# Four value pages of the last group between the passes of the scores in a hybrid decoder step

## The reference

```python
s_past = jnp.einsum('bqhd,bkhd->bhqk', q, k_past) * scale + g[..., :, None] + suffix[..., None, :]
s_new = jnp.einsum('bqhd,bkhd->bhqk', q, k) * scale + g[..., :, None] - g[..., None, :]
s_new = jnp.where(causal, s_new, -jnp.inf)
p = jax.nn.softmax(jnp.concatenate([s_past, s_new], axis=-1), axis=-1)
return einsum('bhqk,bkhd->bqhd', p[..., :n_past], v_past) + einsum('bhqk,bkhd->bqhd', p[..., n_past:], v)
```

## Time and profile before

| | us |
|---|---|
| median of 3 runs | 2198.92 (2190.67 to 2200.44) |
| the profiled execution | 2196.55 |
| its span, first to last instruction | 2194.80 |
| input projection, 0 to 262 | 262 |
| sample attention, 262 to 842 | 580, TensorE busy 477 |
| the rest, 842 to 2195 | 1353, TensorE busy 1293 |

### The profile page before, as it was taken

The page is one execution under the profiler, slowest core; times in us unless marked ns, Lnnn a source line. Parts: engine busy times, 40 slices in busy tenths (PEclk is TensorE's granted clock), DMA queues, the critical chain, the costliest instruction groups (busy, mean ns, idle before and its releaser), DMA issues.

```text
span 2194.8 us, 39552 instructions
## 1 busy us (share of the span) xinstructions
PE 1990.1 (91%) x16059; PEld 1473.1 (67%) x16059; DVE 1047.0 (48%) x1915; ACT 345.6 (16%) x828; POOL 192.4 (9%) x228
## 2 busy tenths in 40 slices
PE   6999588888988677899999998999998899999996
PEld 3778354555555345677777776777776677777774
DVE  5442576666776654533344443304364533344453
ACT  2002122222222111122210001111011122210002
POOL 1400000000000001100002222000001000012220
PEclk9999798999999889999999999999898999999998
DMA  4110698999999994122222223121111122222211
GB/s 169 61 55 4 237 360 317 344 328 357 334 366 350 334 399 173 48 77 77 77 77 77 77 77 115 39 77 39 63 60 49 39 77 78 77 81 81 81 64 43
DMA packets 127602, 320.32 MB, mean 146 GB/s; under 512 B 9852, under 2 KB 10130, under 8 KB 127294
## 3 DMA queue, kind: packets, MB, share of 16 engines
q1 hardware_dynamic: 123874, 304.65, 38.3%
q0 software_dynamic: 3296, 12.98, 1.7%
q10 hardware_dynamic: 252, 0.16, 0.0%
HBM read 309.20 MB, written 8.55 MB: 145 GB/s over the span
## 4 chain that ended last, share of the span: by engine, by line
PE 85%; DVE 4%; issue 4%; DMA 3%; SPq 2%; ACT 1%; ACTq 0%; POOL 0%; DVEq 0%
PE ps L827 51%; PE ps L1005 5%; PE ps L1036 3%; PE ps L1135 3%; PE ps L1136 3%; PE ps L742 1%; PE ps L970 1%; PE ps L743 1%; DMA work<-in_cache_k 1%; PE ps L958 1%; PE ps L959 1%; PE ps L771 1%; PE ps L982 1%; PE ps L772 1%; DMA wring<-in_cache_v 1%
## 5 line engine op out<-in xcount | busy, mean ns | idle before, releaser
L827 PE MATMUL ps<-work 128*128 128x288 f32 x1152 | 296.5, 411 | 12.3 <-DVE work L1636 7.8
L827 PE MATMUL ps<-xn,wring 128*128 128x288 f32 x1008 | 268.8, 410 | 16.7 <-DVE xn L1589 15.7
L827 PEld LDWEIGHTS ps<-work 128*128 128x128 f32 x1152 | 221.6, 193 | 75.5 <-issue 13.6
L827 PE MATMUL ps<-big,wring 128*128 128x288 f32 x944 | 251.5, 410 | 7.6 <-DVE big L2137 7.6
L1853 DVE STREAM_TRANSPOSE work<-work 128x768 f32<-128x768 f32 x256 | 234.5, 954 | 27.1 <-DMA work<-in_cache_k 27.0
L827 PEld LDWEIGHTS ps<-xn,wring 128*128 128x128 f32 x1008 | 193.3, 192 | 71.8 <-issue 16.5
L827 PEld LDWEIGHTS ps<-big,wring 128*128 128x128 f32 x944 | 181.0, 192 | 58.8 <-DVE big L2137 8.5
L1005 PE MATMUL ps<-work,big 32*32 32x256 f32 x6144 | 146.2, 399 | 57.0 <-issue 47.2
L1663 DVE TENSOR_TENSOR work<-ps,work 128x288 f32<-128x288 f32 x72 | 32.9, 458 | 320.8 <-PE ps L827 320.8
L675 POOL TENSOR_TENSOR h<-h,xn 128x288 f32<-128x288 f32 x96 | 106.0, 1106 | 812.5 <-DVE xn L1670 697.7
L1005 PEld LDWEIGHTS ps<-work,big 32*32 32x32 f32 x6144 | 91.6, 105 | 99.3 <-issue 63.6
(11 more groups left out here) (354 smaller groups left out, 2410.4 us busy)
## 6 DMA issues: line engine op xcount, KB each, us to landing
work<-in_cache_k SPq DMA_DIRECT2D x256, 384.0 KB, 7.3
wring<-in_cache_v SPq DMA_DIRECT2D x256, 384.0 KB, 6.2
wring<-in_w_up SPq DMA_DIRECT2D x16, 2048.0 KB, 9.1
wring<-in_w_down SPq DMA_DIRECT2D x16, 2048.0 KB, 7.8
wring<-in_w_in_odd SPq DMA_DIRECT2D x6, 2048.0 KB, 8.0
wring<-in_w_in_even SPq DMA_DIRECT2D x5, 2048.0 KB, 7.9
wring<-in_w_out_odd SPq DMA_DIRECT2D x2, 2048.0 KB, 8.0
big<-in_x_prompt SPq DMA_DIRECT2D x1, 2048.0 KB, 8.8
```

The costliest lines, as they stand in the source:

```text
L827: last = mm(bank, w[:, k, :], x[:, k, :], start=k == 0 and not onto, stop=k == 3, skip_group_check=onto)
```

## The change

In groups 1 to 31 the four value pages 4 to 7 of the last group no longer stand in a row behind the bias run. One page stands behind the second, third, fourth and fifth pass of the scores each. What stood behind them, the prompt step among it, now follows the bias run directly.

```diff
                 for n in range(2 * HC):
+                    if g and n >= 2:
+                        weigh_page(g - 1, GP // 2 + n - 2)
                     score_part(g, n)
                 add_bias(g)
                 if g % GS == GS - 2 and new < NB:
                     turn_new(new)
-                if g:
-                    for p in range(GP // 2, GP):
-                        weigh_page(g - 1, p)
                 if g % GS == GS - 2 and new < NB:
                     weigh_new(new)
                 prompt_step(2 * g)
```

## The result

The changed kernel takes 2227.38 us (median of 4 runs, 2222.53 to 2228.39) beside 2194.80 us for the kernel before on the same chip: 1.0146 times, 95% interval 1.0112 to 1.0179. It is slower by some 32 us, and lies 5 us above the end of the range. The profiled execution took 2226.55 us with a span of 2224.6 us, 29.8 us more than before.

What follows compares the result with a forecast made beforehand. TensorE's own row was taken to set the pace in most groups, with DMA 95% busy. Terms +10 + 7.5 + 2.5 - 12.7 - 6 - 0.6 = +0.7 us on 2196.55 gave 2197 us, no change; range 2174 to 2222.

Steps and rivals of the forecast that it cites:

- The pages in their new place: Score burst, groups 1 to 26: pages standing alone between passes cost 0.40 us more a group, +10 us (-21 to +29).
- The lower end: Score burst: if passes behind pages start as quickly as a burst's first, each group changes by -0.80 us, -21 in all.
- The cover of the softmax: Behind the bias run: without the pages TensorE waits for probabilities in seven groups (4.6 us) and groups 24 to 26 (2.9), +7.5.
- The stops: TensorE's idle "issue" time in score bursts: slower blocks shorten 23 stops by 0.83 us, times 4/6, -12.7 us (0 to -19).
- stops do not shrink: Rival, score burst: the page block moves elsewhere or stops have another cause; 2217 to 2236 us, chance 0.16.
- The clock: TensorE's granted clock in the sample attention: shorter stops bring fewer falls to 1.2 GHz, -6 us (0 to -20).
- The value pages: Inside the bursts: moved pages are wanted earlier, no wait to 0.5 us in each of 26 groups, +2.5 us taken.
- The tail: End of the sample attention: last value pages come sooner, chain ends 2.41 us earlier behind a 1.84 us longer burst, -0.6 us.
- the burst: Sign of being right: from first score to bias run about 1.8 us longer in a group without stops.
- the turn at 3.7 us: Sign of being right: probabilities turned 3.7 us behind the bias run in most groups, with waits for ScalarE in front.
- The issue time in front of scores: Sign of being right: TensorE's "issue" idle time before scores at 30 to 38 us, from 47.2 before.
- The mean clock of 0.94 to 0.95: Sign of being right: TensorE's granted clock over the stretch rises to 0.94 to 0.95, from 0.93.

Runs made afterwards that it cites:

- half pages: Kernel before, but only half of every later cache page is fetched, TensorE's row unchanged: 0.9680 times the time of before.
- The run with the new token later: Changed kernel with the new tokens' multiplies behind the prompt step instead of in front of it: 1.0050 times the time of before.
- pages in a row: Changed kernel with the four pages together behind the last score pass, in front of the bias run: 1.0177 times the time of before.
- eight-column multiplies: Kernel before with an unused multiply of eight columns on a 128x32 tile before the last four passes in 15 groups: 1.0045 times before.
- the prompt's wide multiplies: Kernel before with the prompt's weighted values (L982) moved between third and fourth pass of odd groups' bursts, groups 3 to 25: 0.9920 times before.
- a prompt step put there as well: Kernel with the prompt's wide multiplies in the burst, plus odd groups' second prompt step in the next even group's burst: 1.0065 times before.
- the change and half pages: Changed kernel, but only half of every later cache page is fetched: 0.9823 times the time of before.

## Why the prediction was wrong, point by point

**The pages in their new place** (+10 taken, 16.4 measured). The mechanism and the value were right: 0.46 us to the next pass was taken from the earlier trace rows, and 0.46 is in the timeline. The term itself was sized too small: what is left over, 5.92 - 3.95 - 4 x 0.46 = 0.13 us a burst, and that all 31 groups pay, is the difference. The lower end, a pass that starts quicker behind a page, did not come: the pass behind a page takes 0.67 us.

**The cover of the softmax** (+7.5 taken, +13.9 measured). The step that failed is the sentence that in sixteen groups the turn stands later and keeps its cover: their waits grew by 4.7 us, where the sum had nothing. The seven groups gave 2.9 us for 4.6, groups 24 to 26 3.8 for 2.9, and groups 27 to 30, which the sum left out as hidden, 2.4. (Group 24 is not without prompt work, as the working has it: the prompt's last turn, L970, still stands behind its pages.) I read the delay in the sixteen as a property of the groups. In most of them it was the effect of a stop behind the bias run or of the lower clock, and in several the change takes that away. Group 9 of before, the bias run, the pages and the turn:

```profile
434.96 1.24 PE L1013 MATMUL ps<-xn,c 32*128 32x256 f32 x8
436.13 2.79 PE L1036 MATMUL ps<-wring 128*32 128x192 f32 x32
...
441.91 1.04 PE L1023 MATMUL ps<-c,wring 128*128 128x128 f32 x8
```

The bias run took 1.17 us there instead of 0.64 and the pages 2.72 instead of 1.44, all at the lower clock, and the turn stood at 6.95 us. With half pages and the order of before, where stops are few, it stands at 4.53 us in this group, as in the seven. After the change it stands at 3.75 us in this group and in 18 of the groups 1 to 31 in all, and in all but one of them it waits.

**The new token's wait** (not in the sum, +9.8 us and the prompt step behind it). By the runs this is the largest failure of the working. The prediction named who waits for the exponential and not that seven groups have a second handover between TensorE and VectorE in the same gap, from L1057 over VectorE's copy to L1063, on which the pages had sat as well. With the prompt step queued behind it the price is not 1.4 us but 2.4 us a group in the mean, 3.6 in group 10. The run with the new token later shows it: some 17 to 21 us of the 32, with what hangs on that wait.

**The stops** (-12.7 taken, -29.9 measured). The mechanism was right, and the last section shows it; the size was not. Pages between passes shorten the stop behind them, pages in a row do not (76.6 us), eight-column multiplies do not (77.9), and with half the data in the queues the stops fall to 25.1 and 6.8. The term counted only the stops in front of scores, 47.2 us in the view of waits; those in front of pages, 13.9 us, shrink as well, and in that view both together lose 27.5. And it took 0.83 us from a stop where a burst now lasts 1.97 us longer. The rival "stops do not shrink" gave a range that holds the time, 2217 to 2236, by the wrong mechanism.

**The clock** (-6 taken, up to +15.4 measured). The sign was wrong. I took shorter stops to bring fewer falls, but the granted clock falls behind other waits just as well. In the stretch after the change four spells at 1.2 GHz, 20 us in all, have the new token's wait as the longest pause just in front of them, and four others, 24 us, the softmax wait in groups 25 to 30, which have no prompt step; before, no spell had the first in front of it and two, 14 us, the second in these groups. How much of 112.6 us is lost is not measured by itself; half is the bound.

**The value pages** (+2.5 taken, +3.6 measured). The size was about right, the place was not: all of the 5.3 us now stand inside the bursts, but only 0.9 of them in groups 1 to 26, for which the term was taken, and 4.4 in the bursts of groups 27 to 30.

**The tail** (-0.6 taken). The longer burst came, the earlier end did not. Before, the last step of this chain on TensorE (L1072) stands 11.51 us behind the last bias run:

```profile
839.66 0.47 PE L1072 MATMUL ps<-c,work 128*128 128x128 f32 x1 [1.02 <-DVE work L1907]
```

After the change it stands 868.40 - 858.13 = 10.27 us behind it:

```profile
861.87 1.32 PE L1023 MATMUL ps<-c,wring 128*128 128x128 f32 x8 [3.03 <-ACT wring L1424]
863.22 4.15 PE L1036 MATMUL ps<-wring 128*32 128x192 f32 x64
868.40 0.33 PE L1072 MATMUL ps<-c,work 128*128 128x128 f32 x1 [1.03 <-DVE work L1906]
```

The softmax chain is last, as forecast, but behind its wait of 3.03 us the granted clock falls to 0.5 and the first four pages take twice their time. So 1.2 us are gained here instead of 2.41, and they are lost again further on: from the last bias run to the end of the span it is 2194.80 - 828.15 = 1366.65 us before and 2224.6 - 858.13 = 1366.5 after.

Of the signs that were to show it, the burst (+1.97 for 1.84) and the turn at 3.7 us came as said. The issue time in front of scores fell below the 30 to 38 us, to 27.7. The mean clock of 0.94 to 0.95 did not come, and it is the sign that tells most: 0.90. Two signs of being wrong came: the stretch differs by 27.7 us, and the waits for value pages inside the burst are 5.3 us, over the 5 that were set.

## What to carry to other kernels

Work that is moved out of a gap between a producer and a consumer should be charged with every handover in that gap, and with what is queued behind each; a delay that today covers such a wait counts as cover only if the change does not remove it. To shorten stops in a stream of short instructions, put a few long instructions among them that nobody waits for, as with the prompt's wide multiplies (0.992 times before), not the work that covers another engine; a prompt step put there as well, with VectorE's order left as it was, lost the gain again (1.0065). And when a term promises less idle time, look what the clock does behind the waits that take its place.

## What the runs showed of the hardware that was not expected

Stops at every 256th record depend on the load of the DMA engines: 78.8 us in the stretch at a DMA share of 0.95, 25.1 us at 0.66, with the same instructions on TensorE. That they come from late blocks of instructions can be read directly, since the trace holds the start and length of every packet of q8, one packet of 16 KB for each 256 records in the stretch. Packets of q8 that start in 376.60 to 376.80, inside the stop of group 6, before (packets, MB, share of 16 engines over these 0.20 us):

```profile
q8 instruction: 1, 0.02, 29.1%
```

This one starts at 376.70 and takes 0.93 us, and TensorE's next record starts 1.26 us behind its end, at 378.89. In 34 of the 35 stops before, and in 27 of the 28 after, the next record starts 1.2 to 1.6 us behind the end of such a packet; where TensorE passes a 256th record without a pause, the packet ended 4.0 to 4.3 us earlier in the median. Whenever TensorE passes such a place in these two runs, the block behind it has landed and the one after that has not. With half pages the packet starts 1.5 us behind the 256th record before it (median), with whole pages 3.2.

A wait of 1.75 us for the new token's copy was followed by 3.4 us at 1.2 GHz in group 22 after the change, with no other pause over 0.3 us in the 5 us in front of the fall; the sum had read such a fall only behind a stop of 2.35 us. It is not so each time: with the change and half pages the same wait is followed by such a spell in groups 10, 14, 18 and 22, and not in 2, 6 and 26.

A multiply of eight columns on other tiles costs 0.16 us between two passes, though it computes next to nothing. The Trainium skill says in "TensorEngine Tiling (Array Packing)", Key Properties, that a change of the tiling mode drains TensorE; the trace agrees with these 0.16 us, and with 0.46 us for a page between passes against 0.36 in a row.
